# Two transformer blocks in one kernel: the second block's first projections taken from unnormalised inputs, and the down projection begun on early halves

## Chip, cores and metric

The program runs on one core of one Trainium2 chip. The metric is the device time of one execution in microseconds (us), as the median over runs. All names and line numbers without another remark are those of the kernel before.

## What is computed

Two blocks run one after the other on 512 tokens of width 1024, all in float32. The first (attention of two kinds, then a convolved feed-forward part) ends with a down projection from 2816 to 1024 and a normalised residual. The second starts with a modulated norm and one wide projection:

```
ffn = (gelu(u_gate) * u_val) @ w_down
h = h + rms_norm(ffn, norm_gains[3])                # end of the first block
h2 = rms_norm(h, norm_mix_g) * (1 + sc1) + sh1      # modulate: start of the second
proj = h2 @ w_in                                    # q_a, k_a, v_a, qk_m, v_m, o_m, gates
q, k = rope(rms_norm(q_a, q_g)), rope(rms_norm(k_a, k_g))
```

`sh1` and `sc1` are vectors over the 1024 features, made from a condition by the `w_ada` product. rms_norm scales each token by its rstd, 1/sqrt(mean(x*x) + eps).

## The kernel before

**Layout.** Features lie on the 128 partitions, tokens along the free dimension, so a [1024, 512] activation is eight tiles of 128x512 (index k). Every float32 operand of a projection is split in a high half (rounded to the matmul's fp32r type, by ScalarE) and a low half (the rest, by VectorE), and each product is three matmuls: high x high, high x low, low x high (`three`, L517 to L519). Weights come in chunks through a raw buffer of two slots (SyncE's DMAs); `split(n)` makes chunk n's halves in slot n % 2, first on ScalarE (L1366), then on VectorE (L1991), once the chunk two before is used up (table `USED`). A semaphore counter orders each engine against the others; the order on an engine is the order in which the code is written.

**Up projection.** 44 tiles j, each in two banks, 2*(j % 4) and the next, each 24 x 2 matmuls of 258 columns. VectorE evacuates tile j with rstd (L2286), does a convolution of three taps (L2291 to L2297), and for every second tile multiplies with ScalarE's gelu (L2304) into `aF[:, i, :]`, i = 0 to 21. Between them it makes the `ada` sums (L2198), the product of the condition with `w_ada`; `modulation` (L2204) moves finished ones out of PSUM.

**Down projection.** `down` runs two groups of four output tiles (banks 0 to 3, then 4 to 7) over 11 chunks of two inputs v. `narrow` makes the halves of v in `dh1`, `dl1` (L1631 on ScalarE, L2310 on VectorE), four buffers in turn; they lie in the memory of the convolution's `uc` and `uu`, so all wait for the last `aF`. `free_up` lets TensorE into banks 0 and 4 when all 44 up tiles are evacuated.

**Boundary.** ScalarE squares the eight outputs, VectorE adds the squares (L2000), TensorE sums them over the partitions (`norm_sums`, L560), ScalarE adds eps (L1386), GpSimd takes the power -0.5 (L484), TensorE spreads the result over the partitions (L566), ScalarE copies it to `rst` (L1390). This is norm 3. VectorE then makes the new h (L2340, L2343), and norm 4 goes the same way but with TensorE summing each square itself (`norm_sum_of`, four matmuls of one column per tile, recorded as eight). Then `norm_tiles` makes the normalised and modulated halves `hnh`, `hnl` (L2018 and L2010 on VectorE, L1398 on ScalarE between them), and TensorE multiplies three tiles side by side, one input tile k at a time:

```
for k in range(8):
    pe.wait_ge(S["xl"], 25 + k)
    for b, (x, c) in enumerate(((w2, 0), (w, 0), (w, 128))):
        ins = three(bank(b, T2), ..., hnh[:, k, :], hnl[:, k, :], k == 0, k == 7)
```

A fourth tile from chunk `kq` follows, then the first rope steps: `rope_norm(n)` (L992) sums squares per head, `rope_turn(n)` (L1001) permutes, then the `q3` tile (a fifth of q and k), the spread of k's rstd (L1155), which waits for GpSimd's rope power (L499), and `v5_first`. On ScalarE `evac_q` (L1665) and `rope_square` (L1671) serve them.

## Time and profile before

| | |
|---|---|
| median of 3 runs | 1649.58 us (1648.07 to 1652.67) |
| the profiled execution | 1654.44 us, of it span 1652.7 us |
| TensorE matmuls / weight loads busy | 1545.4 us (94%) / 1381.6 us (84%) |
| VectorE / ScalarE / GpSimd busy | 1016.7 (62%) / 638.8 (39%) / 21.8 (1%) |
| mean granted TensorE clock | 0.961 of full |

The span is cut from the first to the last instruction. A timeline row gives start, duration, engine, line and operation, `out<-in`, how many instructions it merges, and in brackets the idle time before and what ended it. A row of a stretch gives for each engine its busy time and instructions, then PEclk, the granted TensorE clock as a share of full, and the DMA load. TensorE's matmuls overlap their neighbours, so their durations are longer than the distance of their starts.

### The profile page before, as it was taken

How to read it: one execution, taken by the hardware profiler on the slowest of the kernel's cores; microseconds unless marked ns; L12 is line 12 of the kernel's file. 1: busy time of each engine (PE TensorE's matmuls, PEld its weight loads, DVE VectorE, ACT ScalarE, POOL GpSimd, SP SyncE). 2: the span in 40 equal slices, each digit the busy share in tenths (PEclk: the TensorE clock that was granted, in tenths of full speed). 3: DMA queues.
4: the chain of work that ended last, by engine and by line, in shares of the span. 5: the costliest groups of instructions: out<-in, count | busy, mean ns of one | idle time of the engine just before them, and what ended most of it. 6: DMA issues, size and time to landing. Idle time of an engine off the chain costs nothing. (4 is left out here: it accounts for less than half of the span.)

```text
span 1652.7 us, 25815 instructions
## 1 busy us (share of the span) xinstructions
PE 1545.4 (94%) x10752; PEld 1381.6 (84%) x10752; DVE 1016.7 (62%) x1417; ACT 638.8 (39%) x1020; POOL 21.8 (1%) x22
## 2 busy tenths in 40 slices
PE   7999999999998999999899799999877999999996
PEld 7998778888997999999788677767655999998885
DVE  5533445774434777777566545675565888886454
ACT  4423443333323222221343334546543555554342
POOL 0000000000000000000000001000000000000000
PEclk9999998999996999999999789999998999999998
DMA  4221013443220333232344302110102133322332
GB/s 170 101 79 52 13 58 116 147 135 103 96 98 12 115 109 128 96 128 74 124 140 154 105 30 102 52 33 27 39 26 89 52 112 113 109 103 67 100 89 77
DMA packets 37267, 147.61 MB, mean 89 GB/s; under 512 B 4256, under 2 KB 4384, under 8 KB 27296
## 3 DMA queue, kind: packets, MB, share of 16 engines
q1 hardware_dynamic: 37008, 144.92, 26.2%
q8 instruction: 85, 1.39, 0.3%
q0 software_dynamic: 144, 1.05, 0.2%
q14 instruction: 30, 0.25, 0.0%
...
## 5 line engine op out<-in xcount | busy, mean ns | idle before, releaser
L517 PE MATMUL ps<-t 128*128 128x258 f32 (+4 forms) x2144 | 688.3, 321 | 44.0 <-DVE t L2034 10.4
L518 PE MATMUL ps<-t 128*128 128x258 f32 (+4 forms) x2144 | 678.7, 317 | 0.0
L519 PE MATMUL ps<-t 128*128 128x258 f32 (+4 forms) x2144 | 677.3, 316 | 0.0
L517 PEld LDWEIGHTS ps<-t 128*128 128x128 f32 (+1 forms) x2144 | 411.4, 192 | 84.5 <-issue 35.8
L519 PEld LDWEIGHTS ps<-t 128*128 128x128 f32 (+1 forms) x2144 | 411.3, 192 | 26.3
L518 PEld LDWEIGHTS ps<-t 128*128 128x128 f32 (+1 forms) x2144 | 411.6, 192 | 24.3 <-issue 0.2
L1991 DVE TENSOR_TENSOR t<-t 128x2048 fp32r<-128x2048 f32 (+2 forms) x123 | 210.3, 1710 | 239.5 <-ACT t L1366 239.5
L1366 ACT ACTIVATE t<-t 128x2048 fp32r<-128x2048 f32 (+2 forms) x123 | 177.7, 1445 | 186.7 <-PE ps L519 177.2
L1333 PE MATMUL ps<-t 128*128 128x256 f32 x532 | 150.6, 283 | 0.0
L1334 PE MATMUL ps<-t 128*128 128x256 f32 x532 | 150.3, 282 | 0.0
L1335 PE MATMUL ps<-t 128*128 128x256 f32 x532 | 149.1, 280 | 0.0
L1335 PEld LDWEIGHTS ps<-t 128*128 128x128 f32 x532 | 101.2, 190 | 0.0
L1334 PEld LDWEIGHTS ps<-t 128*128 128x128 f32 x532 | 99.8, 188 | 0.0
L1333 PEld LDWEIGHTS ps<-t 128*128 128x128 f32 x532 | 99.5, 187 | 0.0
L2666 DVE TENSOR_TENSOR t<-t 128x1024 fp32r<-128x1024 f32 (+1 forms) x83 | 83.0, 1007 | 21.4 <-ACT t L1919 21.4
L1919 ACT ACTIVATE t<-t 128x1024 fp32r<-128x1024 f32 (+1 forms) x83 | 72.5, 883 | 6.2 <-PE ps L519 3.1
L1622 ACT ACTIVATE t<-t 128x512 f32<-128x512 f32 x22 | 13.9, 632 | 156.5 <-DVE t L2297 156.5
L2198 DVE SCALAR_TENSOR_TENSOR t<-t 128x512 f32<-128x512 f32 x84 | 62.8, 748 | 4.1 <-DMA t<-in_W 0.5
L2286 DVE TENSOR_TENSOR t<-ps,t 128x516 f32<-128x516 f32 x44 | 30.5, 693 | 54.2 <-PE ps L519 49.3
L2310 DVE TENSOR_TENSOR t<-t 128x512 fp32r<-128x512 f32 x88 | 56.6, 685 | 0.6 <-ACT t L1631 0.6
L2654 DVE TENSOR_TENSOR t<-t 128x512 f32<-128x512 f32 x76 | 52.3, 688 | 1.3
L1631 ACT ACTIVATE t<-t 128x512 fp32r<-128x512 f32 x88 | 50.1, 616 | 6.4 <-DVE t L2304 6.4
...
## 6 DMA issues: line engine op xcount, KB each, us to landing
...
```

The lines of the kernel that those rows point to most:

```text
L517: pe.matmul(out, wh, xh, start=first, stop=False)
L518: pe.matmul(out, wh, xl, start=False, stop=False)
L519: return pe.matmul(out, wl, xh, start=False, stop=last)
L1333: pe.matmul(out, wh, xh[:, k, :], start=(k == 0 and b in (0, 1)), stop=False, skip_group_check=True)
L1334: pe.matmul(out, wh, xl[:, k, :], start=False, stop=False, skip_group_check=True)
L1335: ins = pe.matmul(out, wl, xh[:, k, :], start=False, stop=(k == 3), skip_group_check=True)
L1366: ac.activation(whi[:, n % 2, o:o + width], wraw[:, n % 2, 0:width], ACT.Copy).then_inc(S["w_hi"], 1)
L1919: ins = ac.activation(wfh[:, at:at + 512 * len(r)], src[:, a:a + 512 * len(r)], ACT.Copy)
L1991: dv.tensor_tensor(wlo[:, n % 2, o:o + width], wraw[:, n % 2, 0:width], whi[:, n % 2, o:o + width].bitcast(F), ALU.subtract).then_inc(S["w ...
L2198: dv.scalar_tensor_tensor(out=x, in0=raw(n)[:, :], scalar=condc[:, k:k + 1], in1=x, op0=ALU.mult, op1=ALU.add).then_inc(S["a_acc"], 1)
L2310: dv.tensor_tensor(al[v % 4][:, :], src[:, v % 22, :], ah[v % 4][:, :].bitcast(F), ALU.subtract).then_inc(S["an_lo"], 1)
L2666: ins = dv.tensor_tensor(wfl[:, at:at + w_], src[:, a:a + w_], wfh[:, at:at + w_].bitcast(F), ALU.subtract)
```

## The change

1. **Early halves.** The halves of down inputs 0 and 1 get memory outside `uc` and `uu` and are made at the last pair of up tiles; `free_up` waits bank by bank for tiles 40 to 43; the modulation moves from behind the up projection to tile 36. Inputs 2 and 3 still wait for the last `aF`.
2. **Projections from inputs without rstd and shift.** The norm's rstd is one factor per token and the shift one row, so proj = ((h * gm1) @ w) * rstd + sh1 @ w, with gm1 = norm_mix_g * (1 + sc1). The four tiles of chunks `q2` and `kq` are multiplied from `xmh`, `xml`, the halves of h * gm1, made while h is made. VectorE's new `evac_q` multiplies by rstd as it empties the bank. `shift_rows` computes sh1 @ w for the 512 outputs, as products whose weights are the two halves of the shift (`shr`, two columns) and whose moving side is the projection's weights; four small matmuls turn the row into columns, which ScalarE's `evac_q` adds as a bias.
3. **Order.** The sums of norm 4 stand between the products of the merged loop, its spread inside the next tile; chunk `kq` is split ahead of norm 3's eps; `hnh` and `hnl` are still made, behind the first two evacuations, for `q3` and everything later.

```diff
+        shr = sb(s_f, [P, 8, 2], R)
...
-        dh1 = [sb(s_d, [P, T2], R) for _ in range(4)]
-        dl1 = [sb(s_d, [P, T2], R) for _ in range(4)]
+        dh1, dl1 = ([None] * 2 + [sb(s_d, [P, T2], R) for _ in range(2)] for _ in range(2))
+        sb(s_d, [P, 16])
+        for _i in range(2):
+            dh1[_i], dl1[_i] = sb(s_d, [P, T2], R), sb(s_d, [P, T2], R)
...
                         pe.wait_ge(S["up_c"], j - 3)
+                    if j == 40:
+                        pe.wait_ge(S["mod"], 3)
                     if j in (20, 36):
...
             def free_up(b):
-                if b % 4 == 0:
-                    pe.wait_ge(S["up_c"], 44)
-                if b == 1:
-                    pe.wait_ge(S["mod"], 3)
+                if b % 2 == 0:
+                    pe.wait_ge(S["up_c"], 41 + b // 2)
                 if b == 7:
...
+            def shift_rows(z, w):
+                for k in range(8):
+                    pe.matmul(bank(5, 256, slice(0, 2), off=256 * z), shr[:, k, :], w[0][:, k, :], start=(z == 0 and k == 0),
+                              stop=False, skip_group_check=True)
+                    ins = pe.matmul(bank(5, 256, slice(0, 2), off=256 * z), shr[:, k, :], w[1][:, k, :], start=False,
+                                    stop=(k == 7), skip_group_check=True)
+                ins.then_inc(S["mm_q2"], 1)
+            w = weights(AT["q2", 0], 8)
+            pe.wait_ge(S["cst"], 11)
+            pe.wait_ge(S["ev_dn_a"], 3)
+            shift_rows(0, w)
...
+            w2 = weights(AT["kq", 0], 8)
+            shift_rows(1, w2)
+            pe.wait_ge(S["rst"], 4)
+            pe.wait_ge(S["ev_dn_d"], 4)
+            pe.wait_ge(S["ev_dn_a"], 4)
...
-                norm_sum_of(4, 2, k)
-            norm_spread(4, 2)
-            w, w2 = weights(AT["q2", 0], 8), weights(AT["kq", 0], 8)
-            pe.wait_ge(S["rst"], 4)
-            for k in range(8):
+                norm_sum_of(4, 7, k)
...
-                for b, (x, c) in enumerate(((w2, 0), (w, 0), (w, 128))):
-                    ins = three(bank(b, T2), x[0][:, k, c:c + 128], x[1][:, k, c:c + 128], hnh[:, k, :], hnl[:, k, :],
-                                k == 0, k == 7)
+                for b, x in enumerate((w2, w)):
+                    ins = three(bank(b, T2), x[0][:, k, 0:128], x[1][:, k, 0:128], xmh[:, k, :], xml[:, k, :], k == 0, k == 7)
...
+                if k == 2:
+                    pe.wait_ge(S["ev_q2"], 1)
+                    for j in range(4):
+                        ins = pe.matmul(bank(6, 1, off=j), srow[:, 128 * j:128 * j + 128], C("one", 2), start=(j == 0),
+                                        stop=True, skip_group_check=True)
+                    ins.then_inc(S["mm_q2"], 1)
+            for k in range(8):
+                if k == 2:
+                    norm_spread(4, 7)
+                ins = three(bank(2, T2), w[0][:, k, 128:256], w[1][:, k, 128:256], xmh[:, k, :], xml[:, k, :], k == 0, k == 7)
+            ins.then_inc(S["mm_q2"], 1)
...
-            tile(w2, 1, 128, 8, hnh, hnl, 0, (T2,), 3).then_inc(S["mm_q2"], 1)
-            pe.wait_ge(S["ev_dn_d"], 4)
-            pe.wait_ge(S["ev_dn_a"], 4)
+            tile(w2, 1, 128, 8, xmh, xml, 0, (T2,), 3).then_inc(S["mm_q2"], 1)
...
-            tile(w, 0, 128, 8, hnh, hnl, 0, (T2,), 5).then_inc(S["mm_q2"], 1)
+            tile(w, 0, 128, 8, hnh, hnl, 0, (T2,), 5, ("xl", 32)).then_inc(S["mm_q2"], 1)
...
+            ac.activation(shr[:, :, 0], modc[:, 0:8], ACT.Copy).then_inc(S["cst"], 1)
...
-            for i in range(22):
-                if i > 0:
-                    split(AT["up", i] + 1)
-                ac.wait_ge(S["up_u"], 6 * i + 3)
-                ac.activation(uu[0][:, :], uu[0][:, :], ACT.Gelu_apprx_tanh).then_inc(S["up_gl"], 1)
...
-                ac.wait_ge(S[made], v % 22 + 1 if v >= 4 or d == 1 else 22)
+                ac.wait_ge(S[made], 22 if v in (2, 3) and d == 0 else v % 22 + 1)
...
-            for v in range(2):
-                narrow(0, v, dh1, aF, "up_a")
+            for i in range(22):
+                if i > 0:
+                    split(AT["up", i] + 1)
+                if i == 21:
+                    narrow(0, 0, dh1, aF, "up_a")
+                    narrow(0, 1, dh1, aF, "up_a")
+                ac.wait_ge(S["up_u"], 6 * i + 3)
+                ac.activation(uu[0][:, :], uu[0][:, :], ACT.Gelu_apprx_tanh).then_inc(S["up_gl"], 1)
...
+            split(AT["kq", 0])
...
-            split(AT["kq", 0])
...
+                ac.activation(xmh[:, k, :], X(k), ACT.Copy, scale=gm1[:, k:k + 1]).then_inc(S["xh"], 1)
...
-            eps(4, 2)
-            spread(4, 2)
-            apply_norm(2, T2, lambda k: modc[:, k:k + 1], hnh)
+                if k == 1:
+                    ac.wait_ge(S["mm_q2"], 2)
+                    ac.activation(srow, bank(5, T2, slice(0, 2)), ACT.Copy).then_inc(S["ev_q2"], 1)
+                if k == 5:
+                    ac.wait_ge(S["mm_q2"], 3)
+                    ac.activation(bcol[:, :], bank(6, 4), ACT.Copy).then_inc(S["ev_q2"], 1)
+            eps(4, 7)
+            spread(4, 7)
...
-                ac.wait_ge(S["mm_q2"], n + 1)
-                ac.activation(qk2[:, QT[n], :], bank(QB[n], T2), ACT.Copy).then_inc(S["ev_q2"], 1)
+                if n == 4:
+                    ac.wait_ge(S["mm_q2"], n + 4)
+                    ac.activation(qk2[:, QT[n], :], bank(QB[n], T2), ACT.Copy).then_inc(S["ev_q2"], 1)
...
+                c = (2, 0, 1, 3)[n]
+                if n == 0:
+                    ac.wait_ge(S["ev_q2"], 2)
+                ac.wait_ge(S["r_x"], n + 1)
+                ac.activation(qk2[:, QT[n], :], qk2[:, QT[n], :], ACT.Identity, bias=bcol[:, c:c + 1]).then_inc(S["ev_q2"], 1)
...
-                ac.wait_ge(S["ev_q2"], n + 1)
+                ac.wait_ge(S["ev_q2"], n + 3)
...
-            evac_q(0)
-            rope_square(0)
-            split(AT["q3", 0])
-            for n in (1, 2):
+            for n in (0, 1):
...
+            apply_norm(2, T2, lambda k: modc[:, k:k + 1], hnh, 0, 3)
+            split(AT["q3", 0])
+            apply_norm(2, T2, lambda k: modc[:, k:k + 1], hnh, 3, 8)
...
+            evac_q(2)
+            rope_square(2)
...
+            dv.wait_ge(S["cst"], 10)
+            dv.tensor_tensor(shr[:, :, 1], modc[:, 0:8], shr[:, :, 0].bitcast(F), ALU.subtract).then_inc(S["cst"], 1)
+            def narrow(d, v, ah, al, src):
+                dv.wait_ge(S["an_hi"], 44 * d + v + 1)
+                dv.tensor_tensor(al[v % 4][:, :], src[:, v % 22, :], ah[v % 4][:, :].bitcast(F), ALU.subtract
+                                 ).then_inc(S["an_lo"], 1)
...
+                if j == 42:
+                    narrow(0, 0, dh1, dl1, aF)
+                    narrow(0, 1, dh1, dl1, aF)
...
+                if j == 36:
+                    modulation(24, 32, 1, 400, 8)
...
-            modulation(24, 32, 1, 400, 8)
...
-            for v in range(2):
-                narrow(0, v, dh1, dl1, aF)
...
+            split(AT["kq", 0])
+            def xm_low(k):
+                dv.wait_ge(S["xh"], 25 + k)
+                dv.scalar_tensor_tensor(out=xml[:, k, :], in0=X(k), scalar=gm1[:, k:k + 1], in1=xmh[:, k, :].bitcast(F),
+                                        op0=ALU.mult, op1=ALU.subtract).then_inc(S["xl"], 1)
...
-            split(AT["kq", 0])
-            norm_tiles(2, 4, T2, X, lambda k: gm1[:, k:k + 1], lambda k: modc[:, k:k + 1], hnh, hnl)
+                if k >= 1:
+                    xm_low(k - 1)
+            xm_low(7)
+            def evac_q(n):
+                dv.wait_ge(S["mm_q2"], n + 4)
+                dv.tensor_tensor(qk2[:, QT[n], :], bank(QB[n], T2), rst[:, 0:T2], ALU.mult).then_inc(S["r_x"], 1)
+            def hn_tiles(k0, k1):
+                norm_tiles(2, 4, T2, X, lambda k: gm1[:, k:k + 1], lambda k: modc[:, k:k + 1], hnh, hnl, k0, k1)
+            dv.wait_ge(S["rst"], 5)
+            evac_q(0)
+            evac_q(1)
+            hn_tiles(0, 3)
+            split(AT["q3", 0])
+            hn_tiles(3, 8)
+            dv.wait_ge(S["xl"], 40)
...
-            split(AT["q3", 0])
+            split(AT["v5", 0])
...
-            split(AT["v5", 0])
+            evac_q(2)
+            evac_q(3)
...
-            dv.wait_ge(S["r_x"], 1)
+            dv.wait_ge(S["r_x"], 5)
```

VectorE at the end of the up projection, before (L2286 to L2304 are the work on one tile, L1991 a weight split, L2204 the modulation, L2310 the low half of a down input):

```order
L2286 TENSOR_TENSOR t<-ps,t 128x516
L2291 TENSOR_SCALAR t<-t 128x512
L2294 SCALAR_TENSOR_TENSOR t<-t 128x512
L2297 SCALAR_TENSOR_TENSOR t<-t 128x512
L2198 SCALAR_TENSOR_TENSOR t<-t 128x512
L2304 TENSOR_TENSOR t<-t 128x512
L2204 TENSOR_TENSOR t<-ps,t 128x8
L2310 TENSOR_TENSOR t<-t 128x512 x2
L1991 TENSOR_TENSOR t<-t 128x1024
L2310 TENSOR_TENSOR t<-t 128x512 x2
```

The same place in the changed kernel, one tile earlier (L2042 is the weight split, L2334 the low half, L2351 the evacuation of tile 42):

```order
L2369 TENSOR_TENSOR t<-t 128x512
L2042 TENSOR_TENSOR t<-t 128x1024
L2334 TENSOR_TENSOR t<-t 128x512 x2
L2351 TENSOR_TENSOR t<-ps,t 128x516
L2356 TENSOR_SCALAR t<-t 128x512
L2359 SCALAR_TENSOR_TENSOR t<-t 128x512
L2362 SCALAR_TENSOR_TENSOR t<-t 128x512
```

The two low halves now stand ahead of the evacuation of tile 42, and no modulation is left here.

VectorE at the boundary, before (L2340 and L2343 make h, L1991 is the split of chunk kq, L2018 and L2010 the normalised tiles):

```order
L2340 SCALAR_TENSOR_TENSOR t<-t 128x512
L2343 TENSOR_TENSOR t<-t 128x512
L2340 SCALAR_TENSOR_TENSOR t<-t 128x512
L2343 TENSOR_TENSOR t<-t 128x512
L1991 TENSOR_TENSOR t<-t 128x2048
L2018 SCALAR_TENSOR_TENSOR t<-t 128x512 x2
L2010 SCALAR_TENSOR_TENSOR t<-t 128x512
```

And in the changed kernel (L2042 is that split, L2403 and L2406 make h, L2398 the low half of h * gm1):

```order
L2051 TENSOR_TENSOR t<-t 128x512 x3
L2042 TENSOR_TENSOR t<-t 128x2048
L2403 SCALAR_TENSOR_TENSOR t<-t 128x512
L2406 TENSOR_TENSOR t<-t 128x512
L2403 SCALAR_TENSOR_TENSOR t<-t 128x512
L2406 TENSOR_TENSOR t<-t 128x512
L2398 SCALAR_TENSOR_TENSOR t<-t 128x512
L2403 SCALAR_TENSOR_TENSOR t<-t 128x512
L2406 TENSOR_TENSOR t<-t 128x512
```

The split has moved ahead of h, and each tile of h has one more operation behind it.

TensorE at the boundary, before (L560 sums, L566 spread, L517 to L519 a product):

```order
L519 MATMUL ps<-t 128x512
L560 MATMUL ps<-t 128x1 x4
L566 MATMUL ps<-t 128x128 x4
L560 MATMUL ps<-t 128x1 x32
L566 MATMUL ps<-t 128x128 x4
L517 MATMUL ps<-t 128x512
L518 MATMUL ps<-t 128x512
```

And in the changed kernel (L979 and L981 are shift_rows, L571 one sum, L528 to L530 a product):

```order
L979 MATMUL ps<-t 2x256
L981 MATMUL ps<-t 2x256
L571 MATMUL ps<-t 128x1 x4
L528 MATMUL ps<-t 128x512
L529 MATMUL ps<-t 128x512
L530 MATMUL ps<-t 128x512
L528 MATMUL ps<-t 128x512
L529 MATMUL ps<-t 128x512
L530 MATMUL ps<-t 128x512
L571 MATMUL ps<-t 128x1 x4
```

The second spread no longer stands ahead of the products; each input tile has its sum and then two products of three matmuls.

## Rows read from the trace of the kernel before

**Rows 1.** Timeline, TensorE, first down chunk: start us, us, operation, [idle <-releaser].

```profile
795.08 0.77 PE L517 MATMUL ps<-t 128*128 128x512 f32 x1 [5.78 <-DVE t L2310]
795.65 0.63 PE L518 MATMUL ps<-t 128*128 128x512 f32 x1
796.08 0.63 PE L519 MATMUL ps<-t 128*128 128x512 f32 x1
...
802.34 0.40 PE L517 MATMUL ps<-t 128*128 128x512 f32 x1
802.57 0.40 PE L518 MATMUL ps<-t 128*128 128x512 f32 x1
```

**Rows 2.** Timeline, VectorE, end of the up projection.

```profile
783.65 0.70 DVE L2286 TENSOR_TENSOR t<-ps,t 128x516 f32<-128x516 f32 x1 [0.45 <-PE ps L519]
...
789.41 0.69 DVE L2286 TENSOR_TENSOR t<-ps,t 128x516 f32<-128x516 f32 x1 [2.83 <-PE ps L519]
...
792.91 0.68 DVE L2304 TENSOR_TENSOR t<-t 128x512 f32<-128x512 f32 x1
...
794.29 1.29 DVE L2310 TENSOR_TENSOR t<-t 128x512 fp32r<-128x512 f32 x2 [0.62 <-ACT t L1631]
795.76 1.22 DVE L1991 TENSOR_TENSOR t<-t 128x1024 fp32r<-128x1024 f32 x1 [0.17 <-ACT t L1366]
```

**Rows 3.** Stretches; the number after the five engines is PEclk.

```profile
62.00:66.00 4.00, 4.00 (x36) 2.95 (x34) 2.25 (x2) 1.72 (x1) 0.00 (x0) 1.00 0.00 0
516.00:520.00 4.00, 4.00 (x21) 4.00 (x21) 2.12 (x3) 0.54 (x2) 0.00 (x0) 0.50 0.00 0
532.00:534.00 2.00, 2.00 (x17) 2.00 (x18) 0.00 (x0) 0.89 (x2) 0.00 (x0) 0.93 0.00 0
792.00:794.00 2.00, 0.00 (x0) 0.00 (x0) 1.67 (x4) 0.37 (x1) 0.00 (x0) 0.50 0.00 0
937.00:939.00 2.00, 2.00 (x11) 2.00 (x11) 1.93 (x4) 0.92 (x2) 0.00 (x0) 0.50 0.00 0
959.00:961.00 2.00, 2.00 (x10) 1.59 (x10) 1.93 (x4) 1.23 (x2) 0.00 (x0) 1.00 0.00 0
```

**Rows 4.** Timeline, TensorE, boundary of the blocks.

```profile
927.12 1.02 PE L560 MATMUL ps<-t 128*128 128x1 f32 x8 [3.49 <-DVE t L2000]
...
934.75 13.78 PE L560 MATMUL ps<-t 128*128 128x1 f32 x64 [3.09 <-ACT t L1374]
...
955.20 0.77 PE L517 MATMUL ps<-t 128*128 128x512 f32 x1 [3.11 <-DVE t L2010]
...
979.39 0.95 PE L992 MATMUL ps<-t 128*128 128x2 f32 x8
...
986.83 1.09 PE L1155 MATMUL ps<-t 128*64 128x128 f32 x16
```

**Rows 5.** Timelines, ScalarE (one row) and VectorE, boundary of the blocks.

```profile
932.19 1.90 ACT L1366 ACTIVATE t<-t 128x2048 fp32r<-128x2048 f32 x1
...
932.33 0.75 DVE L2340 SCALAR_TENSOR_TENSOR t<-t 128x512 f32<-128x512 f32 x1 [5.36 <-ACT t L1390]
...
943.44 2.28 DVE L1991 TENSOR_TENSOR t<-t 128x2048 fp32r<-128x2048 f32 x1
952.76 1.41 DVE L2018 SCALAR_TENSOR_TENSOR t<-t 128x512 f32<-128x512 f32 x2 [7.04 <-ACT t L1390]
...
963.01 1.63 DVE L2010 SCALAR_TENSOR_TENSOR t<-t 128x512 fp32r<-128x512 f32 x2
```

**Rows 6.** Timelines, GpSimd (three powers) and one VectorE neighbour.

```profile
928.52 1.01 POOL L484 TENSOR_TENSOR t<-t 128x4 f32<-128x4 f32 x1 [386.21 <-ACT t L1386]
...
994.59 1.64 POOL L499 TENSOR_TENSOR t<-t 128x8 f32<-128x8 f32 x1 [3.52 <-ACT t L1676]
1003.24 2.05 POOL L499 TENSOR_TENSOR t<-t 128x8 f32<-128x8 f32 x1 [7.01 <-ACT t L1676]
...
1003.05 0.74 DVE L2356 SCALAR_TENSOR_TENSOR t<-t 128x512 f32<-128x512 f32 x1
```

37 lines of the change are left out of this document (21 added, 16 removed).

## The prediction

> **What bounds the kernel now.** I first read the table of engines: TensorE is busy for 94% of the span, so the end can move only by filling its holes, by taking instructions from it, or by clock. I then read its timeline around the two places that the diff touches, and asked what ended each hole.
>
> The first hole is between the up and the down projection. TensorE's first down product starts at 795.08 after waiting 5.78 us for VectorE [rows 1]; the last up product ended at 789.30, and a product behind it could have started at 789.2, since neighbours overlap. VectorE meanwhile evacuates tile 43, does the convolution and the last product (ends 793.60), a modulation, and only then the subtraction that gives the low half of input 0 [rows 2]. The granted clock falls to 0.50 in that hole (1.2 GHz) [rows 3] and is back at 2.4 GHz a few us into the chunk: 512-column matmuls start 0.43 us apart at 795.65 and 0.23 apart at 802.34. The first chunk of 24 therefore takes 802.34 - 795.08 = 7.26 us instead of 24 x 0.234 = 5.6.
>
> The second hole is the boundary of the blocks. From 923.6 to 955.20 TensorE does only statistics [rows 4]: sums for rstd 3, its spread, 64 one-column passes for the squares of the sum (13.8 us, which is 1.72 us for each of eight tiles, at 0.50 of the clock as the row of 937 shows [rows 3]), another spread, and then 3.11 us of waiting for the first normalised tile. The real projections start at 955.20, cold once more.
>
> **Part one, the early down chunk.** VectorE and ScalarE now make halves 0 and 1 while tile 42 is still multiplied. VectorE had 0.45 us of slack before tile 42's evacuation and 2.83 before tile 43's [rows 2]; two subtractions (1.29 for the pair in the same rows) make tile 42 0.85 late, and tile 43's slack takes that in whole. The modulation goes to tile 36, where it costs 0.16 of an engine that waits anyway. The 24 products of chunk 0 need banks 0 to 3, whose tiles 40 and 41 are evacuated before 783.65, so they follow the last up tile at once, at the full clock: 789.2 + 5.6 = 794.8. Chunk 1 needs half 2, whose memory is still the convolution's, so it waits for the product at 793.60; then come VectorE's split of the weights (first in its queue, a 1.2 us operation [rows 2]), a subtraction of 0.7 and 0.1 of signalling: 795.4. TensorE idles about 0.6 there, which is what is late next. Chunk 1 started at 802.34 and now starts at 795.4: **6.9 us** gained. The other 21 chunks run at TensorE's pace and hand it on.
>
> **Part two, the boundary.** I add up the new path in the old trace's times and leave the 6.9 out.
>
> *To rstd 3.* Sixteen 256-column products with two-column weights (the shift's row) go behind the last down product, from 923.6 for 1.9 us. The sums start only at 927.12, so they cost nothing; without that wait they would cost their 1.9. ScalarE's split of the next weights (1.90 [rows 5]) now stands ahead of the eps and ends at 928.1, when the eps would start anyway. VectorE's half of it runs from 928.05 for 2.3 us, right across GpSimd's power at 928.52. The power alone took 1.01 there, but of the longer ones that at 1003.24 took 2.05 against 1.64 at 994.59, beside a VectorE operation with two SBUF inputs that had 0.55 left [rows 6]: 0.41 more, that is the overlap less some 0.15. An overlap of 1.8 gives **1.65 us late**. Bounds: nothing, and 1.8. If only the largest lateness in a row (0.41) applied, the sum would be 1.2 better; I take the overlap, because the rows grow with it. The Trainium skill, SBUF — State Buffer, "Who interferes with whom", says that such a VectorE instruction and a GpSimd one that reads SBUF exclude each other for a whole instruction; it would give the upper bound, 1.8.
>
> *To the first projection.* The second sixteen shift products follow the spread at the half clock (16 x 0.215 = 3.4) and end at 936.75. The first sum was at 934.75; 1.65 late, and 0.45 later for ScalarE's new high half ahead of the square: 936.8. They fit in just before it.
>
> *The merged loop.* VectorE needs 1.39 per tile (eight from 932.33 to 943.44, the split's start [rows 5]) and now one more operation of 0.66: 2.05. TensorE needs a sum (0.81 at full clock: the eight small passes of 979.39 take 0.95, of which 0.14 overlap the next [rows 4]) and six products (1.40): 2.21. So at the full clock TensorE sets the pace: 8 x 2.21 = 17.7, and four small transposes, 0.8: 955.3. The decisive point is the clock. At the half clock a pass costs 1.72 + 6 x 0.427 = 4.27. I take the full clock. At 955.20 TensorE began unbroken products in the cold, and from 959 on the row shows 1.00 [rows 3, 4]; in the new order the spread and the shift products are unbroken work for 5.5 us, just before the loop. Does a product with two-column weights count? The nearest row is the tile with eight-column weights from 61.6 to 67.4, beside which the clock stayed at 1.00 [rows 3]. Against it speaks the first block's loop, rival 1.
>
> The small new copies (the shift's halves, its row, its columns) stand on ScalarE and VectorE where both wait for TensorE or for each other, and cost nothing; if the loop ran cold, ScalarE's wait for the transposes would hold back tiles 6 and 7, still ahead of TensorE.
>
> *Behind the loop.* The second q2 tile (5.6) with a spread of 1.0 in it ends at 961.9, the second kq tile at 967.5; that was 979.39, so 11.9 earlier. The normalised inputs now come later than the projections, and the q3 tile needs them. Rstd 4 is copied by 958.4; two evacuations on VectorE, then four operations of 0.63 on ScalarE hold the first normalised tile to 961.6; eight tiles at 1.45 us (952.76 to 964.64, where the last pair ends [rows 5]) with q3's split (2.3, a copy and a 1.23 us subtraction) between them end at 974.5, the q3 tile at 975.2 where it could have ended at 974.5. The rope's power starts behind ScalarE's last tile, beside VectorE's, at 974.0 and takes 1.64 to 2.2: the spread of k's rstd starts at 976.2, before at 986.83 [rows 4]: **10.6 us** gained. Another 0.4 goes to q2's evacuations, which now take two engines: 10.2. Attention behind it is as before.
>
> Sum: 6.9 + 10.2 = **17.1 us**. The profiled execution took 1654.44 (span 1652.7, so 1.7 around it), 4.9 above the median; it would become 1637.3, and the median 1649.58 - 17.1 = **1632.5**. The bounds of the small terms (chunk 1 by 0.7 either way, the power 0 to 1.8, the first passes at the lower clock 0 to 3, the order behind the loop by 1.5) give 1629 to 1637.
>
> **Rivals.** 1. *The merged loop runs cold.* In the first block the same kind of loop, 12 products of 258 columns and a sum of 2.1 us per pass, ran at 0.50 while TensorE was 100% busy, and rose only behind 532 (0.93 in that row), after four passes and a half [rows 3]. Here products and sums alternate alike: 2.56 and 1.72 us, there 2.58 and 2.13. For it: those rows. Against it: there TensorE had stood idle before the loop, here it comes from 5.5 us of work. Five cold passes cost 5 x 2.06 and 0.9 for the transposes: 11.2, so 1643.7; fewer passes lie between, all eight give 1649.
> 2. *The power isn't held up*: 1.65 more gain, 1630.9. For it: none of the rows has such a long neighbour.
> 3. *The early chunk only moves the hole.* If half 2 waits for more than the split ahead of it, for instance because tile 42's lateness reaches tile 43, chunk 1 starts up to 1.3 later: 1634. In the extreme chunk 0 doesn't start early at all: 1639.
> 4. *Slower.* The clock stays at 1.2 GHz beyond the loop, through both tiles and q3, because the sums and the transposes leave gaps. The place is 936.8 on: 34.2 + 1.7 + 12.3 + 10.2 + 12.2 = 70.6 us, to 1007.4, against 986.83, less part one's 6.9: 13.7 slower, 1663. Each cold us loses about 0.48, so it decides from some 35 us of cold clock on. Against it: two unbroken tiles of 512-column products lie in that stretch, and with such the clock rose soon behind 955.20 [rows 3, 4].
>
> **How the numbers follow.** Forecast 0.58, rival 1 0.25, rival 2 0.12, rival 3 0.03, rival 4 0.02. The range 1627 to 1645 holds the forecast's own range, rivals 2 and 3 and about two thirds of rival 1, and reaches two us lower since several terms were taken at their cautious end. A measurement of this kernel tells about 0.3%, 4.9 us, from no change: rival 1 with seven or eight cold passes lies within it (0.06), only rival 4 is slower (0.02), and the rest is faster (0.92).
>
> **What would show it.** Right: no TensorE hole over 1 us between the last up tile and chunk 1, the granted clock at 1.00 throughout; GpSimd's first power there at about 2.7 us; the merged loop at some 2.2 us per pass with one-column passes of 0.1 us each; the second kq tile ending about 19 us (11.9 + 6.9) earlier than 979.39. Wrong: one-column passes of 0.2 us and 4.3 us per pass (rival 1), a power of 1.0 (rival 2), a hole of several us ahead of chunk 0 or 1 (rival 3), or a q3 tile that waits more than a us for normalised inputs.

## The result, and the profile after

| | kernel before | changed kernel |
|---|---|---|
| median of ten runs | 1649.71 us (1648.07 to 1657.57) | 1632.54 us (1628.67 to 1644.68) |
| profiled execution, time and span | 1654.44, 1652.7 | 1640.41, 1638.6 |
| its mean granted clock | 0.961 | 0.969 |

The changed kernel takes 0.9905 of the time before, 95% interval 0.9884 to 0.9926: 12 to 19 us less. The forecast was 1632.5. Its single runs lie farther apart than those before, and the longer ones have the lower mean clock: 1628.67 with 0.975, 1644.68 with 0.965. The profiled one is among the longer, 8 us above the median. So what follows compares its stretches, and no totals. One later execution of the changed kernel, a profiled one, was disturbed from end to end (2157 us, mean clock 0.646) and is in no median, range or interval below.

**The end of the up projection.** VectorE's rows of the timeline of the changed kernel (L2334 the low halves, L2351 the evacuation of an up tile, L2369 the last product, L2042 the split of the weights):

```profile
780.55 1.29 DVE L2334 TENSOR_TENSOR t<-t 128x512 fp32r<-128x512 f32 x2
781.76 0.69 DVE L2351 TENSOR_TENSOR t<-ps,t 128x516 f32<-128x516 f32 x1
...
786.85 0.69 DVE L2351 TENSOR_TENSOR t<-ps,t 128x516 f32<-128x516 f32 x1 [2.17 <-PE ps L530]
...
790.35 0.68 DVE L2369 TENSOR_TENSOR t<-t 128x512 f32<-128x512 f32 x1
790.95 1.22 DVE L2042 TENSOR_TENSOR t<-t 128x1024 fp32r<-128x1024 f32 x1
792.09 1.28 DVE L2334 TENSOR_TENSOR t<-t 128x512 fp32r<-128x512 f32 x2
```

and TensorE's, the first product of the down projection and the first one that waits:

```profile
786.58 0.40 PE L528 MATMUL ps<-t 128*128 128x512 f32 x1
...
792.92 0.47 PE L528 MATMUL ps<-t 128*128 128x512 f32 x1 [0.57 <-DVE t L2334]
```

The two early subtractions stand ahead of tile 42's evacuation, which has no slack left, and tile 43 still waits 2.17 us for TensorE (2.83 before, [rows 2]): the lateness was taken in there. The down projection follows the last up product at once. Counted from tile 43's evacuation, chunk 1 starts after 792.92 - 786.85 = 6.07 us, where it was 802.34 - 789.41 = 12.93 [rows 1, 2]: 6.86 less.

**The boundary, up to rstd 3.** ScalarE's and VectorE's halves of the kq split, and GpSimd's power:

```profile
916.73 1.89 ACT L1400 ACTIVATE t<-t 128x2048 fp32r<-128x2048 f32 x1
...
918.65 2.29 DVE L2042 TENSOR_TENSOR t<-t 128x2048 fp32r<-128x2048 f32 x1 [1.04 <-ACT t L1400]
...
919.16 2.65 POOL L495 TENSOR_TENSOR t<-t 128x4 f32<-128x4 f32 x1 [379.40 <-ACT t L1420]
```

The power took 2.65 where it took 1.01 [rows 6]; VectorE's subtraction overlaps it by 1.78.

**From there to the spread of k's rstd.** TensorE's rows: L571 sums of squares (the first is rstd 3's, the others a pass of the merged loop each), L577 a spread, L1028 the pass that follows the second kq tile, L1189 the spread that was L1155:

```profile
917.76 1.02 PE L571 MATMUL ps<-t 128*128 128x1 f32 x8 [1.52 <-DVE t L2051]
921.86 2.08 PE L577 MATMUL ps<-t 128*128 128x128 f32 x8 [3.08 <-POOL t L495]
...
927.56 1.02 PE L571 MATMUL ps<-t 128*128 128x1 f32 x8 [0.99 <-ACT t L1408]
...
930.78 1.70 PE L571 MATMUL ps<-t 128*128 128x1 f32 x8
...
935.05 1.28 PE L571 MATMUL ps<-t 128*128 128x1 f32 x8
...
938.75 1.05 PE L571 MATMUL ps<-t 128*128 128x1 f32 x8
...
941.14 0.95 PE L571 MATMUL ps<-t 128*128 128x1 f32 x8
...
948.00 0.95 PE L571 MATMUL ps<-t 128*128 128x1 f32 x8
...
962.39 0.95 PE L1028 MATMUL ps<-t 128*128 128x2 f32 x8
...
971.01 1.09 PE L1189 MATMUL ps<-t 128*64 128x128 f32 x16 [0.53 <-POOL t L510]
```

Stretches of the same kernel; the number after the five engines is PEclk:

```profile
926.00:928.00 2.00, 1.01 (x9) 0.66 (x8) 1.97 (x4) 1.74 (x3) 0.00 (x0) 1.00 0.73 303
928.00:930.00 2.00, 2.00 (x11) 1.65 (x11) 1.97 (x4) 1.67 (x4) 0.00 (x0) 0.72 0.04 16
930.00:934.00 4.00, 4.00 (x15) 3.52 (x14) 3.93 (x7) 2.49 (x5) 0.00 (x0) 0.50 0.00 0
```

The last five passes follow each other by 2.3 to 2.4 us, near the 2.2 of the forecast. But the clock had risen to 2.4 GHz by 926, and it fell to 1.2 GHz again at 928.9, inside pass 0, and stayed there to about 935.7, with TensorE 100% busy (pass 0 itself had begun behind 0.99 us of waiting); pass 1 took 4.27, and pass 2, with the four transposes behind it, 3.70. From the sums to the spread of k's rstd it is now 971.01 - 917.76 = 53.25 us, before 986.83 - 927.12 = 59.71 [rows 4]: 6.46 less.

The profiled executions differ by 14.1 us in span. Tile 43 was evacuated 2.56 earlier, part one gives 6.86, the boundary 6.46, and 1.8 are lost behind it. The 2.56 are not the change's, and they are a difference of two larger things. The up loop of the first block rose to the full clock after one pass in this execution, and after four and a half in the one before [rows 3]: from the power of rstd 1 to that of rstd 2 it is 30.18 us instead of 39.06. But the power of rstd 1 itself started at 508.42 instead of 502.08, behind code that is the same in both. In all thirteen traces used here it starts between 499.8 and 508.4. Every trace has further stretches at the half clock, ahead of that point and behind the boundary, many of them with TensorE busy all the time; from 990 us on, without the idle end, they add up to 34 us here and to 27 in the kernel before. With the sums of experiment 5 the time from the spread of k's rstd to the end is 665.8 us, and 665.9 before, so the 1.8 us are not a cost of the change either. A single time depends on the clock in many places.

### The profile page after: what moved, and what is told of

Same layout as the page of the kernel before. It is cut to its first block and busy times, and to the rows that moved or that the text cites. A ratio compares the mean times of both kernels' runs of the same rounds, so it can differ in the third digit from the quotient of the medians.

```text
span 1638.6 us, 25916 instructions
## 1 busy us (share of the span) xinstructions
PE 1542.1 (94%) x10792; PEld 1375.9 (84%) x10792; DVE 1024.6 (63%) x1430; ACT 645.1 (39%) x1031; POOL 25.3 (2%) x22
## 3 DMA queue, kind: packets, MB, share of 16 engines
q0 software_dynamic: 144, 1.05, 0.2%
## 5 line engine op out<-in xcount | busy, mean ns | idle before, releaser
L528 PE MATMUL ps<-t 128*128 128x258 f32 (+4 forms) x2144 | 687.9, 321 | 36.5 <-DVE t L2085 11.4
L530 PE MATMUL ps<-t 128*128 128x258 f32 (+4 forms) x2144 | 678.0, 316 | 0.0
L528 PEld LDWEIGHTS ps<-t 128*128 128x128 f32 (+1 forms) x2144 | 411.1, 192 | 76.3 <-issue 26.5
L530 PEld LDWEIGHTS ps<-t 128*128 128x128 f32 (+1 forms) x2144 | 410.0, 191 | 26.0
L2042 DVE TENSOR_TENSOR t<-t 128x2048 fp32r<-128x2048 f32 (+2 forms) x123 | 210.4, 1710 | 227.8 <-ACT t L1400 227.8
L2351 DVE TENSOR_TENSOR t<-ps,t 128x516 f32<-128x516 f32 x44 | 30.4, 692 | 52.6 <-PE ps L530 47.8
L2334 DVE TENSOR_TENSOR t<-t 128x512 fp32r<-128x512 f32 x88 | 56.6, 684 | 0.0
L1999 ACT ACTIVATE t<-ps 128x256 f32<-128x256 f32 x76 | 29.2, 384 | 57.7 <-PE ps L1369 56.9
```

What stands on the lines that cost most here:

```text
L528: pe.matmul(out, wh, xh, start=first, stop=False)
L530: return pe.matmul(out, wl, xh, start=False, stop=last)
L2042: dv.tensor_tensor(wlo[:, n % 2, o:o + width], wraw[:, n % 2, 0:width], whi[:, n % 2, o:o + width].bitcast(F), ALU.subtract).then_inc(S["w ...
L2334: dv.tensor_tensor(al[v % 4][:, :], src[:, v % 22, :], ah[v % 4][:, :].bitcast(F), ALU.subtract).then_inc(S["an_lo"], 1)
```

## The experiments

Twelve more kernels ran (one of them the changed kernel again), in three series of four, each beside the kernel before. For every profiled execution I read the same two intervals, between starts of GpSimd's powers: **A**, rstd 1 to rstd 2, holds the first block's up loop; **B**, rstd 3 to the power of k's rstd, holds the boundary. They are free of what the clock did elsewhere.

B compares only kernels with the same order at the boundary. The last power in it, and the spread that needs its result, in the kernel before (first row; its spread starts at 986.83 [rows 4]) and in the changed one (second row; 971.01):

```profile
980.72 1.64 POOL L499 TENSOR_TENSOR t<-t 128x8 f32<-128x8 f32 x1 [30.76 <-ACT t L1676]
968.90 2.05 POOL L510 TENSOR_TENSOR t<-t 128x8 f32<-128x8 f32 x1 [18.54 <-ACT t L1725]
```

Before, TensorE is still in the q3 tile when the power ends, so 6.11 us pass to the spread; now it waits for the power, and 2.11 pass. Across the two orders I therefore use the **path**, from the sums of rstd 3 to that spread: 59.7 before, 60.0 in part one alone, 55.9 in the kernel before with wide sums, and for all others B and 3.5.

| kernel | median (range), us | kernel before, same series | ratio, 95% interval | A | B |
|---|---|---|---|---|---|
| before | 1649.71 | | | 39.1 | 52.2 |
| changed | 1632.54 (1628.7 to 1644.7) | 1649.71 | 0.9905 (0.9884 to 0.9926) | 30.2 | 49.7 |
| part one alone | 1643.52 (1642.8 to 1647.7) | 1650.92 | 0.9952 (0.9933 to 0.9970) | 32.3 | 52.4 |
| part two alone | 1646.25 (1635.8 to 1654.8) | 1650.92 | 0.9957 (0.9928 to 0.9986) | 30.2 | 57.6 |
| split behind eps | 1636.00 (1633.7 to 1638.6) | 1650.92 | 0.9903 (0.9884 to 0.9922) | 32.3 | 51.8 |
| fillers at the boundary | 1643.13 (1635.3 to 1646.2) | 1650.92 | 0.9936 (0.9912 to 0.9960) | 30.2 | 48.8 |
| changed, again | 1637.79 (1631.7 to 1645.3) | 1649.77 | 0.9928 (0.9903 to 0.9953) | | |
| wide sums, merged loop | 1629.81 (1629.5 to 1639.2) | 1649.77 | 0.9894 (0.9871 to 0.9918) | 32.4 | 46.6 |
| wide sums, up loop | 1634.52 (1628.9 to 1636.9) | 1649.77 | 0.9898 (0.9878 to 0.9917) | 31.3 | 46.8 |
| both wide, split behind eps | 1631.45 (1631.0 to 1632.0) | 1649.77 | 0.9886 (0.9869 to 0.9902) | 31.3 | 46.4 |
| part two alone, wide | 1642.84 (1635.7 to 1650.6) | 1652.04 | 0.9939 (0.9919 to 0.9960) | 39.1 | 46.6 |
| before, wide | 1651.07 (1645.1 to 1657.6) | 1652.04 | 0.9997 (0.9977 to 1.0017) | 39.0 | 48.4 |
| wide in the merged loop, fillers in the up loop | 1630.23 (1626.2 to 1632.5) | 1652.04 | 0.9866 (0.9838 to 0.9895) | 27.9 | 46.6 |
| both wide, fillers in the up loop | 1628.57 (1625.9 to 1632.7) | 1652.04 | 0.9861 (0.9835 to 0.9887) | 27.9 | 46.6 |

(The changed kernel's second series has no usable trace, and so no A and B. Each row of A and B is one execution.)

### 1. Part one alone

The edits to the down projection's start, put into the kernel before:

```diff
-                if b % 4 == 0:
-                    pe.wait_ge(S["up_c"], 44)
-                if b == 1:
-                    pe.wait_ge(S["mod"], 3)
+                if b % 2 == 0:
+                    pe.wait_ge(S["up_c"], 41 + b // 2)
...
+                if j == 42:
+                    narrow(0, 0, dh1, dl1, aF)
+                    narrow(0, 1, dh1, dl1, aF)
```

> The kernel before with the early halves, the freed banks and the moved modulation alone; the boundary of the blocks is as before. My theory (the two parts add, each worth what its own hole gives): chunk 0 follows the last up product at the full clock, chunk 1 starts 0.5 to 1 us after it, and the time is 6.9 us below the kernel before (ratio 0.9958, about 1642.8 against 1649.7). Rival: the early chunk starts early but the down projection is slowed elsewhere, so that less than 3 us come through; then the boundary must have given more than 14 of the 17 us. Other rival: this part gave nearly all of it, above 12 us.

Measured: 7.4 us between the medians, 4.9 to 11 by the interval. The first product that waits, in its trace:

```profile
788.92 0.47 PE L519 MATMUL ps<-t 128*128 128x512 f32 x1 [0.57 <-DVE t L2283]
```

It is the same 0.57 as in the changed kernel, 788.92 - 782.85 = 6.07 us behind tile 43's evacuation, and the clock stays at 1.00 through it. B is as before (52.4 and 52.2). The first term holds by itself, and both rivals are out: less than 3 us, and above 12.

### 2. Part two alone

The changed kernel with those edits undone.

> The changed kernel with its first part undone: halves 0 and 1 made after the product, the down projection waits for tile 43 again. My theory: 10.2 us below the kernel before if the merged loop runs at 2.3 us per pass throughout, less 2 us for each pass that runs at the half clock; the after-trace had about two such, so 6 to 8 below (ratio about 0.9955). The hole of 5.8 us ahead of the first down chunk is back. Rival (the parts interact: the earlier down projection changes what the boundary costs): the two gains of these two kernels don't add up to 17 within 3 us.

Measured: 4.7 us between the medians, anything from 2 to 12 by the interval, and single runs over 19 us. By the medians the two parts sum to 12.1 and the change gives 17.2: beyond the 3 us that I allowed. By the ratios they sum to 15.0 (0.48% and 0.43%) and the change gives 15.7, so no interaction of the parts is shown. What the one trace shows is how far a single execution can be from the forecast. In it the path is 980.12 - 918.99 = 61.1 us, 1.4 *longer* than before, where the forecast had it 10.6 shorter. The clock fell twice in the merged loop (first fence, part two alone; second fence, part two with the wide sums of experiment 5):

```profile
936.00:940.00 4.00, 4.00 (x15) 3.41 (x14) 3.73 (x7) 1.24 (x2) 0.00 (x0) 0.50 0.00 0
940.00:944.00 4.00, 4.00 (x26) 3.18 (x24) 1.31 (x3) 1.30 (x3) 0.00 (x0) 0.93 0.02 4
944.00:948.00 4.00, 4.00 (x15) 3.52 (x14) 1.45 (x2) 1.24 (x2) 0.00 (x0) 0.50 0.00 0
948.00:952.00 4.00, 4.00 (x15) 3.42 (x15) 0.00 (x0) 0.63 (x1) 0.00 (x0) 0.50 0.00 0
```

```profile
940.00:944.00 4.00, 4.00 (x24) 3.18 (x22) 3.93 (x7) 2.38 (x4) 0.00 (x0) 1.00 0.00 0
944.00:948.00 4.00, 4.00 (x31) 3.72 (x30) 3.93 (x7) 2.24 (x5) 0.00 (x0) 1.00 0.02 4
```

So my rival 1 is no mere possibility: the merged loop with its one-column sums is met at 1.2 GHz in most of its passes here, in two or three of them in the after-trace, and in at most the first in one later trace (experiment 6). That makes the clock inside the loop the thing to explain.

### 3. The power without its neighbour

```diff
-            split(AT["kq", 0])
             eps(3, 0)
+            split(AT["kq", 0])
             spread(3, 0)
```

> The changed kernel with ScalarE's split of the kq weights behind the eps instead of ahead of it, so that VectorE's half of it starts about 921 instead of 918.65 and no VectorE operation runs beside GpSimd's power. My theory (the power took 2.65 instead of 1.01 because VectorE's 2.29 us subtraction ran across it): the power takes 1.0 to 1.1, the spread starts 1.6 us sooner after the eps, and since VectorE's split now ends at 923.3 in the times of the after-trace, its first residual product starts 1.3 us sooner; the time falls by 1.3. Rival (the power is longer for a reason of its own, as its place behind other work): it stays at 2.6, and the time rises by about 1 because the split ends later.

The power took 1.01 again, so the neighbour is the cause of the 2.65. But none of the 1.3 us can be seen in the time: 0.9903, the changed kernel had 0.9905. In its own trace the merged loop lost far more to the clock. The sums of passes 4 and 5:

```profile
929.10 1.70 PE L571 MATMUL ps<-t 128*128 128x1 f32 x8
...
933.37 1.70 PE L571 MATMUL ps<-t 128*128 128x1 f32 x8
```

They are 4.27 us apart. The cleaner comparison, one trace against one, is the version with both wide sums and this order, which has no fall in the loop. Its rows of VectorE, GpSimd and TensorE (L572 the sums of rstd 3, L578 the spread, L589 the loop's sums):

```profile
913.15 1.01 POOL L496 TENSOR_TENSOR t<-t 128x4 f32<-128x4 f32 x1 [377.86 <-ACT t L1425]
...
914.21 1.16 PE L578 MATMUL ps<-t 128*128 128x128 f32 x8 [1.44 <-POOL t L496]
914.90 2.29 DVE L2048 TENSOR_TENSOR t<-t 128x2048 fp32r<-128x2048 f32 x1 [3.30 <-ACT t L1405]
...
920.71 1.71 PE L589 MATMUL ps<-t 128*128 128x128 f32 x8
```

Its B is 46.4, against 46.6 with the old order: the power ends 1.6 sooner, and 0.2 is left of it. VectorE's split ends at 917.2, and the second shift products need it. TensorE idles from 915.4 until then, the clock drops to 1.2 GHz, the sixteen products run at it past the point where the first square is ready, and pass 0 starts cold (1.71 for its eight passes). What is late next had changed from the power to the split's end, and the clock had fallen in the gap that it left.

### 4. Matmuls that only keep TensorE busy

```diff
             shift_rows(0, w)
+            warm(AT["q2", 0], 5, 3)
...
             norm_sums(3, 0)
+            warm(AT["q2", 0], 14, 3)
             norm_spread(3, 0)
...
             shift_rows(1, w2)
+            warm(AT["q2", 0], 4, 3)
```

`warm(n, m, b)` is m matmuls of 512 columns of the weights n into bank b.

> The changed kernel with 5, 14 and 4 matmuls of 512 columns, whose result nothing reads, in TensorE's three idle gaps at the boundary: ahead of the sums of rstd 3, ahead of its spread, and behind the second shift products. My theory (the granted clock fell in the idle time ahead of the spread, and again in the first passes of the merged loop): the spread takes 1.0 instead of 2.08 us, the shift products are 0.11 apart, all eight passes take 2.2 to 2.3, so the loop ends about 4.5 us earlier than in the after-trace, and the time falls by 3 to 5 us where the loop had cold passes. Rival A: the clock falls in the loop all the same, because the one-column sums themselves lower it; then the fillers bring 1 us or nothing. Rival B: the fillers run over the gaps' ends and cost what they last, up to 2 us slower.

The median is 1643.13, ratio 0.9936, the interval overlapping that of the changed kernel: no gain, and rival A. Rival B is out in this trace: the first sum of the loop starts 922.94 - 914.04 = 8.90 us behind those of rstd 3, 0.9 sooner than in the after-trace, so the fillers held nothing up. Stretches, and the sums of passes 0, 3 and 4:

```profile
918.00:922.00 4.00, 4.00 (x30) 2.89 (x28) 1.99 (x3) 1.05 (x2) 0.76 (x2) 1.00 0.75 255
...
926.00:930.00 4.00, 4.00 (x24) 3.19 (x23) 3.93 (x7) 2.38 (x5) 0.00 (x0) 1.00 0.01 4
930.00:934.00 4.00, 4.00 (x22) 3.52 (x22) 3.93 (x7) 2.41 (x5) 0.00 (x0) 0.75 0.00 0
934.00:938.00 4.00, 4.00 (x15) 3.50 (x14) 2.32 (x4) 1.24 (x2) 0.00 (x0) 0.50 0.00 0
```

```profile
922.94 1.02 PE L571 MATMUL ps<-t 128*128 128x1 f32 x8 [0.84 <-ACT t L1417]
...
930.95 1.05 PE L571 MATMUL ps<-t 128*128 128x1 f32 x8
...
934.44 1.70 PE L571 MATMUL ps<-t 128*128 128x1 f32 x8
```

The loop was entered at the full clock, after some 8 us of nearly unbroken work and 0.84 of waiting, ran three passes at 2.3 us, and the clock fell at 932, with TensorE 100% busy. My prediction turned on the state in which the loop is entered; this trace shows that a loop entered at the full clock can lose it all the same.

### 5. The same sums, 128 columns wide

```diff
-                col_stat(sq[k % 2][:, 0:NORM_N[i]], NORM_N[i], b, k == 0, C("o1024")[:, 0:1]).then_inc(S["col"], 1)
+                for j, (a, _) in enumerate(col_tiles(NORM_N[i])):
+                    ins = pe.matmul(bank(b, SUM_W[i], off=SUM_W[i] * j), sq[k % 2][:, a:a + 128],
+                                    C("o1024")[:, 0:1].to_broadcast([P, SUM_W[i]]), start=(k == 0 and j == 0), stop=True,
+                                    skip_group_check=True)
+                ins.then_inc(S["col"], 1)
```

> The changed kernel with the sums of squares of the merged loop 128 columns wide instead of one: the same 64 passes, each result repeated in 128 columns, and ScalarE's eps reads every 128th. My theory (the clock falls in the merged loop, with TensorE busy all the time, because 0.95 us of each 2.28 us pass move one column each; both the after-trace and the run with fillers fell there): no fall inside the loop, all eight passes take 2.3 to 2.4 us, 18.9 for the loop against 22.7 in the after-trace, and the median is 2 to 5 us below that of the changed kernel in the same call. A 128-column pass costs nearly what a one-column pass costs (the spread's eight took 1.05 us, the sum's eight 1.02). Rival A (it falls whatever the width): cold stretches in the loop again, 0 to 1 us slower. Rival B (wide passes are dearer than I read): passes of 2.7 us and more, about 3 us slower.

The sums of passes 0, 1 and 7, the spread of k's rstd, and a stretch of the loop:

```profile
921.68 1.13 PE L589 MATMUL ps<-t 128*128 128x128 f32 x8 [0.63 <-ACT t L1413]
...
924.05 1.05 PE L589 MATMUL ps<-t 128*128 128x128 f32 x8
...
938.98 1.05 PE L589 MATMUL ps<-t 128*128 128x128 f32 x8
...
961.99 1.09 PE L1194 MATMUL ps<-t 128*64 128x128 f32 x16 [0.53 <-POOL t L511]
```

```profile
932.00:936.00 4.00, 4.00 (x28) 3.55 (x27) 3.27 (x5) 2.47 (x4) 0.00 (x0) 1.00 0.00 0
```

No fall, passes of 2.3 us, and the width costs nothing that can be seen: B is 46.6, and 46.8 with narrow sums in the one execution where these kept their clock (the next experiment's). The loop takes 19.6 us with the transposes, forecast 18.9. In its own series this kernel is at 1629.81, four of its six runs within 0.5 us of each other, the unaltered change at 1637.79: 8.0 us, more than the 2 to 5 forecast. By the two ratios the gain is 5.6 us, with an uncertainty that reaches from 0 to 11, and against the first ten runs of the change (0.9905) it is 1.8: the size is less certain than the effect on the clock. The other two runs, at 1636.54 and 1639.18, have the lower mean clocks (0.971 and 0.969 against 0.976); without traces of them I can't say where they lost it. For the effect I go by all the traces: with narrow sums the merged loop fell in four of five (changed, part two alone, split behind eps, fillers), with wide ones in none of five. Each of those is one execution, of kernels that differ in more than the width; if the width did nothing, four falls in the five narrow ones and none in the wide would come about by chance once in some 40 times.

What TensorE did just before the five falls was alike in all of them: some 2.0 us made of one-column sums together with a wait or with the transposes. In the after-trace (fall at 928.9) and once in part two alone (930.3) that was 0.9 to 1.0 us of waiting and the 1.0 of pass 0's sums; in part two alone again (943.9), with the split behind eps (928.4) and with the fillers (932.0) it was the four small transposes, 1.05, and pass 3's sums directly behind them. The clock fell 0 to 1.4 us behind their end, and in none of these traces right behind a pass whose sums (0.95 us) stood between products on both sides. But three more such stretches of 1.9 to 2.0 us had no fall behind them (the transposes of the after-trace, those of the next experiment's kernel, pass 0 with the fillers), so that being there doesn't decide by itself: five of eight. I haven't tried to move the transposes or the wait with narrow sums; which of the three matters is open, the timing of the falls is all there is for it, and only the width of the sums was put to the test.

### 6. The unaltered change beside it, and the up loop's sums

> The changed kernel unaltered, beside the three that follow, on the same chip. Its ten runs so far lie in two groups, 1628.7 to 1632.9 and 1640.4 to 1644.7, with mean granted clocks of 0.973 to 0.975 and 0.965 to 0.969. My theory (one or two stretches at the half clock come or stay away by chance) expects both groups again; a rival (something of the chip or the day) expects one of them.

Its five other runs are 1631.65, 1636.51, 1637.79, 1641.19 and 1645.29, with clocks from 0.974 to 0.967: a spread rather than the two groups that I expected. The traces show at least three places that differ from execution to execution: the start of rstd 1's power (499.8 to 508.4), the up loop (A) and the merged loop (B). Over the fifteen runs of the unaltered change the merged loop's share of the spread isn't known.

The up loop of the first block, 96 columns wide (`SUM_W = (1, 1, 96, 1, 1, 1, 1)`):

> The changed kernel with the sums of squares of the first block's up loop (80 one-column passes beside 96 products of 258 columns) 96 columns wide. The loop of the kernel before took 4.71 us per pass for four and a half passes at the half clock, that of the changed kernel one such pass. My theory: the rise comes after one pass at the latest, so that this loop costs the same as in the after-trace (0 to 1 us of gain) and the runs of the slower group become rarer if they came from here. Rival (the rise depends on the time alone, not on what the sums move): cold stretches of up to four passes in some runs, no gain in the median.

A is 31.3, between the 30.2 and the 32.4 of most narrow loops (39 in three traces): nothing seen. The median of 1634.52 is below the 1637.79 beside it, but the intervals overlap by a third; it decides nothing, all the more since in its trace the merged loop happened to keep its clock.

> Both wide sums and the split of the kq weights behind the eps. My theory: the gains add: 1.3 for the power and 2 to 5 for the merged loop, so 3 to 6 us below the changed kernel of the same call, near 1627, and no fall of the clock between 925 and 948. Rival: the clock that one loop keeps, another stage loses again; then the median lies within 2 us of the changed kernel and the cold time in the trace is as long as before, at other places.

1631.45, 6.3 below the change of the same series and above the 1627 that I gave; against the wide merged loop alone 1.6 more by the medians and 1.3 less by the ratios, so no difference. Four runs within 1 us. No fall between 925 and 948, as the theory had it, but the half clock from 915.4 to 922, see experiment 3. The gains don't add, because that of the power isn't there.

### 7. Part two with the loop's clock held

> The second part of the change alone, with the sums of the merged loop 128 columns wide, so that its passes keep one clock. My theory (the prediction's second term, 10.2 us, holds where the loop is warm, and the chance of cold passes alone made the narrow version lie anywhere between 1635.8 and 1654.8): about 1650 less 10 to 14, so 1636 to 1640, with a spread between runs that is half that of the narrow version. Rival (the second part is worth 5 to 7 us whatever the loop's clock, and the other kernels gained by an effect of the first part on the boundary): 1643 to 1645.

9.2 us between the medians, 10.1 by the ratio (6.6 to 13.4): between the 10 to 14 forecast and the rival's 5 to 7, which the interval just touches. The trace is clearer: B is 46.6 and the path 50.1, both as with part one in place, so no effect of part one on the boundary is seen. The spread between the runs is 15 us, not half of 19, so most of it isn't the merged loop's; in this trace A is 39.1, the up loop having been at the half clock for four passes and a half, which is one place where the rest can come from. To add up, the sum of the parts belongs beside the whole change with wide sums: by the ratios 7.9 and 10.1 make 18.0, against 17.5; by the medians 16.6 against 20.0. Within these uncertainties the parts add.

### 8. The kernel before with wide sums

> The kernel before with its 64 one-column passes of the second norm 128 columns wide, at their old place ahead of the projections. Here the sums are TensorE's only work and it waits for ScalarE and VectorE between them. Theory A (the width alone is enough to bring the clock up): the eight tiles take 11.1 us at VectorE's pace of 1.39 instead of 13.8, the spread 1.0 instead of 2.0, and the projections start warm, 4 to 6 us gained without moving any product. Theory B (what keeps the clock in the merged loop is the products; wide sums only tip the balance): the clock stays at 0.50, the passes take 1.7 to 1.9 us, no change or up to 1 us slower.

```profile
938.09 7.86 PE L578 MATMUL ps<-t 128*128 128x128 f32 x48 [3.10 <-ACT t L1379]
946.18 1.16 PE L578 MATMUL ps<-t 128*128 128x128 f32 x8 [0.23 <-ACT t L1379]
947.57 1.16 PE L578 MATMUL ps<-t 128*128 128x128 f32 x8 [0.23 <-ACT t L1379]
...
950.21 1.16 PE L567 MATMUL ps<-t 128*128 128x128 f32 x8 [1.48 <-POOL t L485]
954.47 0.76 PE L518 MATMUL ps<-t 128*128 128x512 f32 x1 [3.11 <-DVE t L2016]
```

The clock did rise during the sums, 64 passes took 10.6 us instead of 13.8, the spread 1.16; then came the 3.1 us wait for the first normalised tile, and the projections began cold as before. B is 3.8 shorter, just under the 4 to 6 that theory A gave, and theory B is out; but A's warm start of the projections is missing, and in the median nothing of the gain can be told (0.9977 to 1.0017). In that trace 3.5 us were lost again behind B: it is at the half clock from about 1088.6 to 1092 and from 1139.8 to 1143.2, places where the kernel before ran at the full clock, with the same instructions. Holding the clock in the sums doesn't replace the change, which takes away the wait and the second cold start.

### 9. Fillers in the first block

```diff
+            pe.wait_ge(S["w_lo"], split_count(AT["up", 0]))
+            warm(AT["up", 0], 9, 7)
             norm_sums(1, 4)
+            warm(AT["up", 0], 6, 7)
             norm_spread(1, 4)
+            warm(AT["up", 0], 19, 7)
```

> The changed kernel with the wide sums of the merged loop and, in the first block, 9, 6 and 19 unread matmuls of 512 columns in TensorE's idle gaps ahead of the sums of rstd 1, ahead of its spread, and between the spread and the up loop. Theory: the spread takes 1.3 instead of 2.3 us and the first pass of the up loop 2.6 instead of 4.7, so 2 to 3 us below the version with the wide sums alone (1629.8): about 1627. Rival A (as at the boundary: the narrow sums of the up loop lower the clock later in it, since it is the loop and not the start that decides): cold stretches inside the loop and a median at or above 1630. Rival B: fillers that overrun cost 1 to 2 us.

> The same with the sums of the up loop 96 columns wide too. Theory (start and loop both matter): no stretch at the half clock from 500 to 535, and the narrowest spread between runs of all versions; 80 passes cost at most 0.02 us more each, 1.6 in all, so 1626 to 1629. Rival: a cold stretch in that loop as before, at 1630 or above.

The second version, the sums and spread of rstd 1, the first sums of the up loop, and a stretch of the loop:

```profile
499.42 1.28 PE L572 MATMUL ps<-t 128*128 128x1 f32 x10
502.31 1.28 PE L578 MATMUL ps<-t 128*128 128x128 f32 x10
...
509.48 1.25 PE L595 MATMUL ps<-t 128*128 128x96 f32 x10
```

```profile
508.00:512.00 4.00, 4.00 (x35) 4.00 (x35) 3.93 (x7) 2.38 (x4) 0.00 (x0) 1.00 0.00 0
```

Here the fillers do what they failed to do at the boundary. A is 27.9 in both, with narrow sums and with wide, against 30.2 to 39.1 without. In this loop 12 products of 258 columns and 1.27 us of sums alternate, without transposes or waits between them, and once up, its clock fell in none of the thirteen traces, narrow or wide. So the start decided there, and the width showed nothing. The ratios of the two versions (0.9866, 0.9861) are the lowest of all; against the wide merged loop alone (0.9894) the intervals overlap. The medians, 1630.23 and 1628.57, are 3 us above the 1627 forecast for the first and inside the 1626 to 1629 for the second. The first is also at the 1630 that its rival A gave, but not for the rival's reason, since its loop has no stretch at the half clock. Two forecasts for the second failed: 530 to 534 is at the half clock, just behind the loop, and its runs spread over 6.9 us, where those of the experiment with both wide sums spread over 1.0. By A the fillers are worth 2.3 us in a good execution and 11 in a bad one. The last version is the fastest that I found, 23 us below the kernel before, and 7 below the change by the ratios (0.9861, 0.9905), though not told apart from its neighbours.

## Why the prediction was right, and where not

**Part one, 6.9 us.** Right in size and by its steps: 6.86 in the trace, 7.4 in the median; no wait ahead of chunk 0, tile 43's slack took in tile 42's lateness, the new idle time is 0.57 where I gave 0.6, and the granted clock is 1.00 from 784 to 800. Rival 3 is out.

**The power, 1.65 us late.** 2.65 - 1.01 = 1.64, for an overlap of 1.78; experiment 3 took the neighbour away and the power went back to 1.01. Extending rows of 0.41 to an overlap four times as long was right, and rival 2 is out. By the rule of the Trainium skill, SBUF — State Buffer, "Who interferes with whom", the two exclude each other for a whole instruction, and the trace agrees: the power ends 0.87 us behind the end of the subtraction, so nearly all its 1.01 lies behind it. What I had wrong, in rival 2, is what a power of 1.01 is worth: in experiment 3 0.2, not 1.65, since the split comes out late instead. (There the order had to change for it; a power that stays undisturbed in the old order has no run.)

**The first sum.** 9.7 us behind rstd 3's sums by forecast (936.8 - 927.12), 9.80 in the after-trace and in that of the wide sums.

**The merged loop, 2.21 per pass at the full clock.** 2.29 measured where warm, wide or narrow; that is 0.08 in eight passes, 0.6, and the transposes came to 1.0. From the first sum to the spread of k's rstd the wide version takes 961.99 - 921.68 = 40.3 where the forecast had 976.2 - 936.8 = 39.4, and most of the 0.9 is the loop's. Its boundary is 59.71 - 50.11 = 9.6 us shorter than before, the forecast of the path being 10.6. Two slips in the working matter little: the eight normalised tiles took 11.88 / 8 = 1.49 us each in the rows, not 1.45, and rival 1 with all eight passes cold comes to 1649.9 by its own terms, not 1649.

**"I take the full clock", with 1.00 throughout as its sign, is the step that failed.** I argued from what TensorE does ahead of the loop. The after-trace had the clock up there and lost it in pass 0, and 3.1 us with it (B of 49.7 against 46.6); experiment 4 entered the loop at the full clock and lost it in pass 3. With the products and the order as they are, the width of the sums inside the loop made the difference. Rival 1 had the right price (4.27 per pass, met in four traces) and the wrong picture: cold from the start and rising once, as in the first block. In fact the clock comes and goes, and forecast and rival are both met, in different executions of nearly the same kernel: the merged loop cost 0.2 to 11 us (B of 46.8 to 57.6). A chance of 0.25 for cold passes was too low for single executions, four of five traces showed some, though only one as many as five.

**The products with two-column weights** did not keep the clock down: it rose during the second shift products, at about 925.4, behind a spread of 2.08 us and eight of them. **Behind the loop** all came as forecast: the q3 tile is held up by about 0.65 us (8.62 from the pass ahead of it to the spread, of which 0.53 is the wait for the power, against 7.44 before [rows 4]), where I gave 0.7, and k's power takes 2.05 beside VectorE, inside the 1.64 to 2.2. The slower rival, cold beyond the loop, was seen nowhere.

**The sum.** 6.9 + 10.2 = 17.1 against 17.2 in the medians is closer than the terms deserve, and in part luck: the path of the second is 9.6 us shorter at the full clock and 6.5 in the after-trace, the ratio of the same ten runs gives 15.7, and the five later runs have a median 5 us above the forecast.
